# Merging the split matmuls of the RWKV chunks: 64 columns instead of 32, and 128 instead of 64

## The reference, cut to what matters

```
def step(S, inp):
    r_t, w_t, k_t, v_t, a_t, b_t = inp
    sa = jnp.einsum('bhvk,bhk->bhv', S, a_t)
    S = (S * w_t[:, :, None, :] + sa[..., None] * b_t[:, :, None, :]
         + v_t[..., None] * k_t[:, :, None, :])
    return S, jnp.einsum('bhvk,bhk->bhv', S, r_t)

_, y = lax.scan(step, jnp.zeros((B, H, N, N), jnp.float32), xs)
```

## Time and profile before

| | |
|---|---|
| median of three runs | 3307.14 us |
| lowest and highest | 3306.46 and 3308.02 us |
| the profiled execution's own time | 3308.02 us |
| span in its profile | 3306.2 us |
| TensorE matmul busy | 3172.0 us, 96% of the span |
| VectorE busy | 1732.3 us, 52% |
| ScalarE busy | 1071.4 us, 32% |
| mean granted TensorE clock | 0.988 |

### The profile page before, as it was taken

How to read it: one execution, slowest core, us unless ns; L and a number is a source line. 1 busy time by engine, 2 the same in 40 slices (tenths; PEclk the granted TensorE clock), 3 DMA queues, 4 the chain that set the end, 5 groups by cost and what they waited for, 6 DMA issues and landing times. The chain is left out here.

```text
span 3306.2 us, 57729 instructions
## 1 busy us (share of the span) xinstructions
PE 3172.0 (96%) x24360; PEld 2530.7 (77%) x24360; DVE 1732.3 (52%) x2638; ACT 1071.4 (32%) x1567; POOL 150.9 (5%) x204
## 2 busy tenths in 40 slices
PE   6999899989999999999999999999999999899998
PEld 5777667777776677788887668888888887588887
DVE  6756764565546644643335875333533247863324
ACT  4442223334433222333322443332233223533321
POOL 1000000010000000000001000000000000000000
PEclk9999999999999999999999999999999999999999
DMA  6223222222221111322232212223222322123232
GB/s 231 83 90 104 78 72 98 102 94 83 96 84 67 64 53 66 111 93 100 93 113 77 90 52 96 96 96 115 90 96 96 111 82 96 45 83 102 96 109 77
DMA packets 83554, 304.10 MB, mean 92 GB/s; under 512 B 9680, under 2 KB 9952, under 8 KB 83296
## 3 DMA queue, kind: packets, MB, share of 16 engines
q1 hardware_dynamic: 78064, 283.11, 25.2%
q0 software_dynamic: 5232, 17.31, 1.6%
HBM read 295.66 MB, written 4.72 MB: 91 GB/s over the span
## 5 line engine op out<-in xcount | busy, mean ns | idle before, releaser
L583 PE MATMUL bank<-hh,whi 128*128 128x512 f32 (+1 forms) x2704 | 1067.9, 395 | 32.6 <-DVE hl L1270 9.5
L584 PE MATMUL bank<-hl,whi 128*128 128x512 f32 (+1 forms) x2704 | 1030.1, 381 | 0.0
L585 PE MATMUL bank<-hh,wlo 128*128 128x512 f32 (+1 forms) x2704 | 1029.7, 381 | 0.0
L1270 DVE TENSOR_TENSOR wlo<-raw,whi 128x1024 fp32r<-128x1024 f32 x498 | 610.4, 1226 | 757.0 <-ACT whi L2218 700.5
L2218 ACT CAST whi<-raw 128x1024 fp32r<-128x1024 f32 x498 | 523.7, 1052 | 747.9 <-PE bank L585 681.3
L583 PEld LDWEIGHTS bank<-hh,whi 128*128 128x128 f32 x2704 | 514.8, 190 | 159.9 <-issue 37.1
L585 PEld LDWEIGHTS bank<-hh,wlo 128*128 128x128 f32 x2704 | 514.9, 190 | 98.4
L584 PEld LDWEIGHTS bank<-hl,whi 128*128 128x128 f32 x2704 | 516.3, 191 | 85.8 <-issue 2.4
L583 PE MATMUL bank<-whi,fh 128*128 128x512 f32 x704 | 274.5, 390 | 0.0
L585 PE MATMUL bank<-whi,fl 128*128 128x512 f32 x704 | 274.0, 389 | 0.0
L584 PE MATMUL bank<-wlo,fh 128*128 128x512 f32 x704 | 274.0, 389 | 0.0
(11 more groups left out here) (340 smaller groups left out, 3315.6 us busy)
## 6 DMA issues: line engine op xcount, KB each, us to landing
raw<-in_W SPq DMA_DIRECT2D x514, 512.0 KB, 3.3
bc<-in_ln_g POOLq DMA_DIRECT2D x6, 512.0 KB, 4.1
bc<-in_ln_b POOLq DMA_DIRECT2D x6, 512.0 KB, 5.7
xn<-in_x SPq DMA_DIRECT2D x4, 512.0 KB, 10.0
mrg<-in_W SPq DMA_DIRECT2D x2, 1024.0 KB, 13.4
AR<-in_W SPq DMA_DIRECT2D x2, 1024.0 KB, 17.5
xn<-in_x POOLq DMA_DIRECT2D x4, 512.0 KB, 5.2
xd<-xn POOLq DMA_DIRECT2D x4, 512.0 KB, 3.5
```

The costliest lines, as they stand in the source:

```text
L583: e.matmul(out, ah, bh, start=first, stop=False, skip_group_check=True)
L584: e.matmul(out, ah, bl, start=False, stop=False, skip_group_check=True)
L585: return e.matmul(out, al, bh, start=False, stop=last, skip_group_check=True)
L1270: return self.e.tensor_tensor(o, a, b, op)
```

## The change

The two column halves of each product with U become one matmul of 64 columns, and the same with X. The two runs become one loop, in which a product with U and a product with X alternate. In `from_state` the two 64-column halves of each product become one matmul of 128 columns.

```
         def from_state(bank, j):
             self.wait_ge(("cs", at))
-            for t, q in itertools.product(range(2), (0, 64)):
-                a = (2 * g + t) * 1024 + j * 512 + c * 128 + q
-                e.matmul(bank[q:q + 64, t * 128:(t + 1) * 128], k.AR[:, a:a + 64], S0[:, t * 128:(t + 1) * 128], start=t == 0,
-                         stop=False, skip_group_check=True)
+            for t in range(2):
+                a = k.AR[:, (2 * g + t) * 1024 + j * 512 + c * 128:(2 * g + t) * 1024 + j * 512 + (c + 1) * 128]
+                e.matmul(bank[:, t * 128:(t + 1) * 128], a, S0[:, t * 128:(t + 1) * 128], start=t == 0, stop=False,
+                         skip_group_check=True)
...
         self.wait_ge(("cWW", at), ("cXX", at), ("cX", at))
-        for i, q in itertools.product(range(4), (0, 32)):
-            e.matmul(bank[q:q + 32, i * 64:(i + 1) * 64], U[0:64, i * 64 + q:i * 64 + q + 32], Y[0:64, 256 + i * 64:320 + i * 64],
-                     start=True, stop=True, skip_group_check=True)
-        for i, q in itertools.product(range(4), (64, 96)):
-            t = e.matmul(bank[q:q + 32, i * 64:(i + 1) * 64], X[:, i * 64 + q - 64:i * 64 + q - 32], Y[:, 256 + i * 64:320 + i * 64],
-                         start=True, stop=True, skip_group_check=True)
+        for i in range(4):
+            o = slice(i * 64, (i + 1) * 64)
+            e.matmul(bank[0:64, o], U[0:64, o], Y[0:64, 256 + i * 64:320 + i * 64], start=True, stop=True, skip_group_check=True)
+            t = e.matmul(bank[64:128, o], X[:, o], Y[:, 256 + i * 64:320 + i * 64], start=True, stop=True, skip_group_check=True)
         t.then_inc(*self.up(("cS", at)))
```

## The result

The changed kernel takes 3324.74 us (median of 4 runs, 3320.69 to 3328.18) where the kernel before takes 3307.20. The ratio, taken over all 14 runs of the changed kernel, is 1.0056 (1.0043 to 1.0068): 18.5 us slower, 14 to 22, which puts it at 3325.7 us. The forecast was 10.9 us slower, with a range up to 3325. The direction was right, and so was the cause (a change of the array's shape costs time); its price was set too low, and the part that was to be hidden was not. The profiled execution took 3326.05 us, its span is 3324.3 us, 18.1 above the one before.

The account below looks back on a forecast made before the run. TensorE, busy for 96% of the span, was taken as the bound: +9.9 us for cS and +3.1 for from_state make 13.0, less 2.5 hidden, +10.5 us, so 3318 us. The range for 8 in 10 was 3305 to 3325.

Parts of the forecast that it names:

- That a change of shape costs: On TensorE, changing the addressed rows or columns between matmuls was put at about 0.12 us around the change.
- Rival A: In cS, 64-row and 128-row matmuls in separate columns run side by side: cS 0.59 us, time 3301 us; chance 10%.
- Step 1: The step cS, 16 times: eight alternating blocks take 1.76 us where 1.14 stand, +9.9 us on TensorE.
- Steps 2 and 3: from_state's merged matmuls in cW (bank 0, +1.4 us) and cY (bank 1, +2.2 and -0.5 us): together +3.1 us.
- What hides: Of 13.0 us added on TensorE, 2.5 us were to vanish in its waits for VectorE.
- B: TensorE's waits take most of the cost up: +13 on the engine, at most +5 on the time, 3312 us; chance 15%.
- C: In cS each block waits out its last record: 0.27 us a block, 2.19 for eight, time 3325 us; chance 10%.
- rival D: TensorE's clock: shorter waits may avoid one or two low-clock stretches, 2 to 4 us back, 3315 us; no chance given.

Follow-up runs that it names:

- Run 4: Kernel before with cS alternating in 64-column matmuls, products with U reading all 128 rows (a wrong product), from_state unchanged: 3299.06 us, ratio 0.9972.
- run 3: Kernel before with cS merged to 64-column matmuls but grouped, four with U then four with X, from_state unchanged: 3307.40 us, ratio 0.9999.
- run 5: Kernel before with cS alternating in 64-column matmuls, U padded by zeros to 128 rows (right product), from_state unchanged: 3297.24 us, ratio 0.9971.
- Run 8: Kernel before with from_state in 128-column matmuls, moved right behind large matmuls in cW and cY, cS unchanged: 3305.75 us, ratio 0.9995.
- Run 9: Kernel before plus four alternating 64-column matmuls per piece, right ahead of the wait for U at line 935: 3312.91 us, ratio 1.0018.

## Why the prediction was wrong in size

**That a change of shape costs, in both directions and whether or not the columns are disjoint:** right. Run 4 takes only the change of rows away and cS falls from 2.06 to 0.61 us; run 3 takes away six of the seven changes inside cS with the matmuls left as they are. Rival A (the alternation is free) was worked out rightly for 0.59 us, but the trace shows it only with one shape (0.61, runs 4 and 5). What the 0.14 us of a block are made of, no run separates. The timeline with the weight loads shows one thing: among equal shapes a load starts ahead of its matmul, and at a change it does not. The load of line 585 starts 0.23 us before its matmul (285.45), those of lines 1010 and 1011 with theirs (285.76 and 286.02):

```profile
285.22 0.19 PEld L585 LDWEIGHTS bank<-hh,wlo 128*128 128x128 f32 x1
285.76 0.19 PEld L1010 LDWEIGHTS bank<-Y,U 64*64 64x64 f32 x2 [0.35 <-issue]
286.02 0.19 PEld L1011 LDWEIGHTS bank<-Y,X 128*64 128x64 f32 x2
```

**Step 1, the price of a block: the term that failed.** I put 0.22 us where 0.257 was measured, +9.9 us for +14.7. I had fitted "steps plus 0.10" on the 0.56 us of line 994 in the earlier trace rows. But there line 994 follows line 979, of its own shape, so that block contains a way out and no way in. Every block of the alternation has both. With a change ahead of it the same line takes 0.61 us in the changed kernel. The other fit that stood beside it, line 1009 with 0.13 from the earlier trace rows, has both ends; it gave 0.25 a block, 1.97 us and +13.3 us, and I chose the other for its columns. The measured price of a block is 0.14 + 0.058 a record.

**Steps 2 and 3:** +3.1 us for +5.3. The same kind of miss: the way out of the wide group, from its last record to the next shape, was put at 0.15 us and is 0.21 (0.53 less three steps of 0.107). That makes 0.34 for 0.28 in cY with c = 1 and 2, where the way in was right at 0.26. In cW (0.12 for 0.20) line 979 takes 0.15 us longer than before, and line 994 another 0.05 for its way in, which I had left out. Where a large matmul stands ahead (c = 3), I saw a gain of 0.12 us: half of it is not there (0.23 + 0.53 for 0.70), and the way into line 1030 takes the rest. Run 8 shows the reading behind it right: the wide form costs nothing beside its own shape.

**What hides: failed, 2.5 us for nothing.** The time alone can't tell (20.0 less 2.5 would lie in its interval), but the waits can: they did not shrink (47.9 us for 46.3). They are real, but they are on work that VectorE begins when it has this piece's result. In the first piece with c = 1 the transposes at line 935 start 10.81 us after the end of cS before, and 11.19 after the change, 0.38 more, nearly all of it the 0.34 of from_state in between; and they wait for VectorE 1.95 us in both. VectorE's last wait ahead of them is for the bank of cY, before (line 1841) and after (line 1839):

```profile
385.88 0.42 DVE L1841 TENSOR_REDUCE hs<-bank 128x4 f32<-128x256 f32 x1 [0.43 <-PE bank L1032]
389.94 0.43 DVE L1839 TENSOR_REDUCE hs<-bank 128x4 f32<-128x256 f32 x1 [0.79 <-PE bank L1030]
```

From there VectorE has no gap until it has written U, and the transposes start 7.02 us later before and 7.03 after. A later cS moves VectorE's work and the end of the wait together. Run 9 adds the time behind that release and ahead of the wait, and there 4.7 us of 16.5 vanish in it, just as the sizes of the waits say. So waits do hide work, by place: the prediction says itself that VectorE shifts with cY where it waited for the end of cY, and I still gave half of it away.

**Rivals B and C.** B (the waits take most of it up) is out by the same waits. C forecast 3325 us, and that is nearly the measured time, but its mechanism is not what the trace shows: it has each block wait until its last record is done, 0.27 us a block and 2.19 for cS. Measured are 0.257 and 2.06, and the next block starts before the records of the last one end (285.76 + 0.32 is 286.08, line 1011 starts at 286.02). That C's sum comes near is luck: it has 16.8 us for cS and 3.1 for from_state, less 2.5 that are hidden, where 14.7 and 5.3 were measured and nothing was hidden.

**The clock (rival D):** it is a width, not a cause. In the changed kernel's 14 runs the mean clock lies between 0.986 and 0.991; the four at 0.990 or 0.991 took 3320.7 to 3324.3 us, the six at 0.986 or 0.987 3326.9 to 3330.9. The stretches below the full clock follow the same pauses as in the earlier trace rows. The windows of PE there, after the change:

```profile
396.00:400.00 4.00, 1.64 (x34) 0.74 0.28 113
400.00:404.00 4.00, 3.99 (x103) 0.50 0.01 4
404.00:408.00 4.00, 4.00 (x42) 0.50 0.21 74
```

In the profiled run the six among the pieces lose about 17 us of full clock where before loses 15. Why they last longer in one run than in another was not tried.

The three misses have one sign: 13.0 us forecast on TensorE for 20.0 measured, and 2.5 us of cover for none. The prices are the larger part, 7.0 us, of which 4.8 are the block of cS.

## What to carry to other kernels

Count the changes of array shape, not only the matmuls: here each block of small matmuls cost 0.14 us on top of its records, so half the instructions took nearly twice the time. Order small matmuls so that equal shapes (rows and columns) stand together, put a wide one beside wide ones, and where two kinds must alternate give both the same number of rows, if need be with zeros, and different columns, so that they run side by side. When a price is fitted on a block in a trace, look at what stands on both sides of it; and time is hidden by a wait only if it stands between what releases the other engine and the wait itself.

## What was not expected of the hardware

Two column tiles of 64 give twice the rate of one for the same records (0.029 and 0.058 us a record, runs 4 and 3), and one tile of 64 columns does in 8 records what two of 32 do in 16 in about the same time (1.21 and 1.14 us for cS), so merging two narrow matmuls into one that fills a single tile gains nothing. Four records of 128*128 with 128 moving elements begin 0.11 us apart, eight of 128*64 0.055: here, too, the merge only halves the count.

Not every difference in the printed shape is a change that costs. The small matmuls of lines 716 and 717 have a stationary operand 2 columns wide and stand between 128*128 ones; in the kernel before, line 583 starts 0.23 us behind line 717, as it does behind its own shape, where 0.32 lie ahead of a 64*32:

```profile
467.25 0.40 PE L717 MATMUL bank<-wlo,c 128*2 128x512 f32 x1
467.48 0.39 PE L583 MATMUL bank<-hh,whi 128*128 128x512 f32 x1
```

Where between 2 and 32 columns the price begins was not tried.
